# Block 2's mixer: two steps of the delta rule in turns 7 to 11, the end reordered, and products of constants in front of TensorE's waits

## Time and profile before

| | us |
|---|---|
| median of 3 executions | 3647.48 (3641.82 to 3655.58) |
| the profiled execution: its time | 3662.31 |
| its span, first to last instruction | 3660.5 |
| TensorE (PE) busy | 3531.4 |
| VectorE (DVE) busy | 2143.4 |
| ScalarE (ACT) busy | 1253.5 |
| GpSimd (POOL) busy | 699.6 |
| mixer of block 2, pass 1 and pass 2 | 153.9 and 143.9 |

### The profile page before, as it was taken

The page is one execution under the profiler, slowest core; times in us unless marked ns, Lnnn a source line. Parts: engine busy times, 40 slices in busy tenths (PEclk is TensorE's granted clock), DMA queues, the critical chain, the costliest instruction groups (busy, mean ns, idle before and its releaser), DMA issues. The chain is left out here.

```text
span 3660.5 us, 43323 instructions
## 1 busy us (share of the span) xinstructions
PE 3531.4 (96%) x17650; PEld 2759.1 (75%) x17650; DVE 2143.4 (59%) x2908; ACT 1253.5 (34%) x1836; POOL 699.6 (19%) x414
## 2 busy tenths in 40 slices
PE   8999998999999999998999999999999999999999
PEld 6888743788878888744888877686888876768887
DVE  6655556765475556557755577674544565745444
ACT  3222235422243223235422244344222343542221
POOL 3342002244304341002344205100000020000000
PEclk9999999999999999999999999998999999999999
DMA  5443301343433443211444322101233321012332
GB/s 178 142 133 124 106 28 36 135 138 130 133 100 127 136 139 114 91 44 53 139 141 133 124 81 76 35 14 64 87 101 97 96 81 35 14 65 86 101 101 81
DMA packets 97957, 351.16 MB, mean 96 GB/s; under 512 B 11808, under 2 KB 12064, under 8 KB 96864
## 3 DMA queue, kind: packets, MB, share of 16 engines
q1 hardware_dynamic: 97760, 348.40, 29.1%
HBM read 345.86 MB, written 2.42 MB: 95 GB/s over the span
## 5 line engine op out<-in xcount | busy, mean ns | idle before, releaser
L417 ACT ACTIVATE w_hi<-raw 128x1024 fp32r<-128x1024 f32 (+2 forms) x538 | 556.5, 1037 | 1810.5 <-PE ps L336 1727.2
L334 PE MATMUL ps<-xs_hi,w_hi 128*128 128x512 f32 x2304 | 908.0, 394 | 2.5 <-DVE arena L1304 2.5
L336 PE MATMUL ps<-xs_hi,w_lo 128*128 128x512 f32 x2304 | 900.4, 391 | 0.0
L335 PE MATMUL ps<-xs_lo,w_hi 128*128 128x512 f32 x2304 | 900.4, 391 | 0.0
L427 DVE TENSOR_TENSOR w_lo<-raw,w_hi 128x1024 fp32r<-128x1024 f32 (+2 forms) x538 | 673.5, 1253 | 167.9 <-ACT w_hi L417 167.4
L334 PEld LDWEIGHTS ps<-xs_hi,w_hi 128*128 128x128 f32 x2304 | 434.9, 189 | 105.7 <-issue 15.4
L335 PEld LDWEIGHTS ps<-xs_lo,w_hi 128*128 128x128 f32 x2304 | 434.7, 189 | 93.3 <-issue 3.6
L336 PEld LDWEIGHTS ps<-xs_hi,w_lo 128*128 128x128 f32 x2304 | 434.7, 189 | 91.0
L334 PE MATMUL ps<-hd_hi,w_hi 128*128 128x512 f32 x1280 | 500.9, 391 | 2.1 <-DVE hd_lo L1041 2.1
L336 PE MATMUL ps<-hd_hi,w_lo 128*128 128x512 f32 x1280 | 498.7, 390 | 0.0
L335 PE MATMUL ps<-hd_lo,w_hi 128*128 128x512 f32 x1280 | 498.5, 389 | 0.0
(11 more groups left out here) (479 smaller groups left out, 4200.9 us busy)
## 6 DMA issues: line engine op xcount, KB each, us to landing
raw<-in_ffn_gu SPq DMA_DIRECT2D x264, 512.0 KB, 3.8
arena<-in_ada SPq DMA_DIRECT2D x64, 768.0 KB, 5.7
raw<-in_ffn_dn SPq DMA_DIRECT2D x96, 448.0 KB, 3.4
raw<-in_in_t SPq DMA_DIRECT2D x60, 512.0 KB, 3.6
raw<-in_ffn_dn SPq DMA_DIRECT2D x48, 512.0 KB, 3.6
raw<-in_out SPq DMA_DIRECT2D x32, 512.0 KB, 3.6
raw<-in_pleg SPq DMA_DIRECT2D x16, 512.0 KB, 3.6
raw<-in_in_r SPq DMA_DIRECT2D x8, 512.0 KB, 3.6
```

Of the source, the lines that this page charges most:

```text
L334: T.matmul(bank, lhs_hi(k), rhs_hi(k), start=(first and k == 0), stop=False)
L335: T.matmul(bank, lhs_hi(k), rhs_lo(k), start=False, stop=False)
L336: mm = T.matmul(bank, lhs_lo(k), rhs_hi(k), start=False, stop=(last and k == kt - 1))
L417: A.activation(self.hi[:, n % HL, 0:size], raw[:, n % RAW, 0:size], ACT.Copy).then_inc(self.high_done, 1)
```

## The change

1. `weave` takes two delta steps instead of one in each of turns 7 to 11, on all engines. From turn 12 on delta step t + 5 stands in turn t, so the recurrence stands in turns 20 to 27 instead of 25 to 32, and the weave ends after turn 30 (ScalarE's and VectorE's last unit), not 32.
2. Head pairs of the HGRN output are issued alternately (heads 0 and 1 of a pair, product by product) in two turns, 27 and 28, instead of four.
3. `idle_products(bank, n)` multiplies constants into a free PSUM region. It is added after attention units 0 and 2 (512 columns), before levels 9 to 13 (256 columns), before the last z and before U and W (512 columns), and before each chunk's `v_ready` wait (384 columns).
4. The four spreads of steps 2 and 4 are issued before the wait for `kb_ready`.
5. The last chunk's state product and state update are dropped; the state is not used after it.
6. ScalarE: the copies and squares of the HGRN outputs move in front of the SiLUs, which become its last work of the stage; `ring.high` moves up. The squares of the delta output are made chunk by chunk in the mixer (into `o_sq`), so `LateDelta` has no squares left to make. VectorE's `ring.low` calls come one turn earlier.

```diff
-            T.matmul(bank, C("ident"), cst[:, 0:S], start=True, stop=True)
+            T.matmul(bank, C("ident"), cst[:, 0:bank.shape[1]], start=True, stop=True)
...
+    TWICE = range(7, 12)
     def weave(first, second):
         live = [first, second]
+        turn = 0
         while live:
             live = [g for g in live if next(g, DONE) is not DONE]
+            if turn in TWICE:
+                next(first)
+            turn += 1
...
+                    if m in (0, 2):
+                        idle_products(ps[3][:, :], 1)
...
                 for g in range(len(steps)):
-                    pe.wait_ge(x_ready, 2 * g + 3)
...
                     if g >= 2:
                         pe.wait_ge(lev_copied, 2 * (g - 2) + 2)
+                    if g >= 9:
+                        idle_products(ps[2 * (g % 2)][:, 2 * P:S], 1)
+                    pe.wait_ge(x_ready, 2 * g + 3)
...
-                for hd in range(H):
-                    c, e = divmod(hd, 2)
-                    if e == 0:
-                        pe.wait_ge(off_copied, 8 if c else 5)
...
+                for c in range(2):
+                    pe.wait_ge(off_copied, 8 if c else 5)
+                    pair = [(2 * c + e, ps[c][r, :]) for e, r in enumerate(heads_of)]
+                    v_ = lambda hd, j: vn[:, j, P + hd * HD:P + (hd + 1) * HD]
+                    for hd, out in pair:
+                        T.matmul(out[:, 0:P], v_(hd, 0), diag[:, hd, 0, :], start=True, stop=True)
+                    for hd, out in pair:
+                        T.matmul(out[:, P:2 * P], v_(hd, 0), off[:, hd, 0:P], start=True, stop=False)
...
+                    mm.then_inc(o_done, 1)
                     yield
...
             def hgrn_act(act):
...
+                ring.high(act, n0)
                 yield
-                yield
+                act.wait_ge(z_done, 2 * (NL - 1))
+                for c in range(2):
+                    ring.high(act, n0 + 1 + c)
+                    act.wait_ge(o_done, c + 1)
+                    A.activation(hg[:, c, :], ps[c][:, :], ACT.Copy).then_inc(o_copied, 1)
+                    act.wait_ge(o_copied, c + 1)
+                    A.activation(hg_sq[c], hg[:, c, :], ACT.Square)
+                    yield
                 act.wait_ge(lev_done, 4 * NL)
                 for c in range(2):
                     A.activation(hg_gates[:, c, :], bg[:, c, :], ACT.Silu)
                     A.activation(cgt[:, c, :], cgt[:, c, :], ACT.Silu)
-                yield
...
             def hgrn_dve(dve):
...
-                for _ in range(4):
+                for _ in range(3):
                     yield
                 for c in range(3):
                     ring.low(dve, n0 + c)
...
             def delta_pe(pe):
...
                     pe.wait_ge(nat_copied, 4)
-                    pe.wait_ge(kb_ready, 2)
                     if c:
                         pe.wait_ge(head_ready, 4)
                     for e in range(2):
                         T.matmul(ps[6 + e][:, :], pick(4, 2 * c + e), rowG[R4, :], start=True, stop=True).then_inc(spread, 1)
+                    pe.wait_ge(kb_ready, 2)
...
+                        if v == NL - 1:
+                            idle_products(ps[6][:, :], 1)
...
+                idle_products(ps[4][:, :], 1)
                 pe.wait_ge(t_updated, 2 * NL)
...
+                    idle_products(ps[6][:, P:S], 1)
                     pe.wait_ge(v_ready, 2 * j + 2)
...
-                    for hd in range(H):
-                        mm = T.matmul(ps[6][heads_of[hd % 2], (hd // 2) * HD:(hd // 2 + 1) * HD], kdec[:, j, hd * HD:(hd + 1) * HD],
-                                      vnew[:, hd, :], start=True, stop=True)
-                    mm.then_inc(k_done, 1)
+                    if j < ST - 1:
+                        for hd in range(H):
+                            mm = T.matmul(ps[6][heads_of[hd % 2], (hd // 2) * HD:(hd // 2 + 1) * HD], kdec[:, j, hd * HD:(hd + 1) * HD],
+                                          vnew[:, hd, :], start=True, stop=True)
+                        mm.then_inc(k_done, 1)
...
             def delta_act(act):
...
                      .then_inc(out_copied, 1)
+                    act.wait_ge(out_copied, j + 1)
+                    A.activation(o_sq[:, :, j * P:(j + 1) * P], o[:, :, j * P:(j + 1) * P], ACT.Square)
...
             def delta_dve(dve):
...
                     yield
+                    if j == ST - 1:
+                        break
                     dve.wait_ge(k_done, j + 1)
```

More of the change, by code:

```diff
@@ L1079, in program, with __init__ @@
     class LateHeads:
-        def __init__(self, st, x, gains, space, squared=0):
-            self.norms = HeadNorms(st, "late_head", x, gains, HD, space, ps[0], squared=squared)
+        def __init__(self, st, x, gains, space, squares=None):
+            self.norms = HeadNorms(st, "late_head", x, gains, HD, space, ps[0], squares=squares)
             self.gate_ready, self.ready = st.sem("late_gate"), st.sem("late_ready")
@@ L2130, in program, with __init__ @@
     class HeadNorms:
-        def __init__(self, st, tag, x, gains, width, space=None, bank=ps[6], after=None, squared=0):
+        def __init__(self, st, tag, x, gains, width, space=None, bank=ps[6], after=None, squares=None):
             self.x, self.gains, self.width, self.n, self.bank = x, gains, width, len(x), bank
-            self.squared = squared
+            self.squared = len(squares) if squares else 0
             self.squares_before = after.squares_before + after.n - after.squared if after else 0
-            self.sq, self.root, self.rstd = ((space.get(len(x), S), space.get(S), space.get(S)) if space
-                                             else (head_sq, head_root, head_rstd))
+            self.sq = squares or [a[:, r, :] for a in (space.get(len(x), S) if space else head_sq,) for r in range(len(x))]
+            self.root, self.rstd = (space.get(S), space.get(S)) if space else (head_root, head_rstd)
             self.rows = slice(0, 2 * self.n)
@@ L2713, in hgrn_pe @@
                     yield
-                for hd in range(H):
-                    c, e = divmod(hd, 2)
-                    if e == 0:
-                        pe.wait_ge(off_copied, 8 if c else 5)
[L2718 to L2726, removed]
-                    mm = T.matmul(out[:, 3 * P:S], v_(3), diag[:, hd, 3, :], start=False, stop=True)
-                    if e:
-                        mm.then_inc(o_done, 1)
@@ new lines, in hgrn_pe @@
+                for c in range(2):
[6 more added lines that the diff above has]
+                        T.matmul(out[:, P:2 * P], v_(hd, 0), off[:, hd, 0:P], start=True, stop=False)
+                    for hd, out in pair:
+                        T.matmul(out[:, P:2 * P], v_(hd, 1), diag[:, hd, 1, :], start=False, stop=True)
+                    for hd, out in pair:
+                        T.matmul(out[:, 2 * P:S], v_(hd, 0), off[:, hd, 2 * P:4 * P], start=True, stop=False)
+                    for hd, out in pair:
+                        T.matmul(out[:, 2 * P:S], v_(hd, 1), off[:, hd, 4 * P:6 * P], start=False, stop=False)
+                    for hd, out in pair:
+                        T.matmul(out[:, 2 * P:3 * P], v_(hd, 2), diag[:, hd, 2, :], start=False, stop=False)
+                    for hd, out in pair:
+                        T.matmul(out[:, 3 * P:S], v_(hd, 2), off[:, hd, P:2 * P], start=False, stop=False)
+                    for hd, out in pair:
+                        mm = T.matmul(out[:, 3 * P:S], v_(hd, 3), diag[:, hd, 3, :], start=False, stop=True)
+                    mm.then_inc(o_done, 1)
@@ L3118, in _ @@
                 weave(delta_dve(dve), overlapped(window_dve(dve), hgrn_dve(dve)))
-        return X_AT + 6 * S, hg, hg_gates, o, cgt
+        return hg_sq + [o_sq[:, c, :] for c in range(2)], X_AT + 8 * S, hg, hg_gates, o, cgt
     one_half = [0.5] * DT
```

19 lines of the change are left out of this document (5 added, 14 removed).

## The result

The changed kernel takes 3661.2 us (median of 19 runs, 3650.9 to 3666.4), the kernel before 3649.8 (19 runs, 3641.8 to 3658.2). The ratio is 1.0026, with a 95% interval of 1.0019 to 1.0033: about 10 us slower, and the interval leaves out 1. That is under the half percent that the prediction called no change, and inside its range, 3 us under the upper end. Ratios leave out executions that ran at a low clock throughout: there were two, both of the kernel of experiment 10. The profiled execution of the changed kernel took 3659.65 us with a span of 3657.9.

The account below looks back on a forecast made before the run. TensorE bounds it (busy 3531.4 of 3660.5 us). Turn 2 -4.8 and pass 1 without its fall -10.9 give -15.7; falls +12 each, at one and a half +2.3: 3649, no change. Own range 3637 to 3662; with rivals 3626 to 3664.

Parts of the forecast that it names:

- Turns 7 to 11, to W, to the sums: Mixer stretches per pass: 34.1 us, then 31.4 to the end of W (fall adds 12), then 33.9 to the sums.
- The wait in turn 16: TensorE idles 1.65 us before the level in turn 16, as VectorE's delays from GpSimd's copies and a scaling add.
- I take three of four: Share of passes whose clock falls in turns 17 to 19, costing 12 us each.
- The prediction's line for two falls, +8.3: Both mixer passes together, if the clock falls in both: 8.3 us slower than before.
- the idle time of 1.06 led to a fall: Turn 21 before the change: this wait led to a fall in one of two passes; 1.65 should more often.
- Turn 2: Spreads moved ahead remove VectorE's waits for the scores, 2.21 and 2.60 us: -4.8 us over both passes.
- I cost them at nothing: Two products of constants near turn 2, 0.89 us each, taken as covered; if not, +1.8 us a pass.
- The output pairs: HGRN output: four heads take some 4.8 us, not 8.8, but the gain lands behind ScalarE; TensorE idles 5.6.
- 99.4 against 99.4: nothing: Pass 2 from turn 7 to the sums of squares: 99.4 us before and after, no gain.
- Rival 1: 512-column products carry the clock over the half steps; neither pass falls: -19.3 us, 3628; chance 0.20.
- Rival 2: Low clock lasts past W to the off-diagonal products, +10 us a pass more: 3676, or 3664 with one pass; chance 0.10.
- Rival 3: Output pairs don't overlap, each pass loses 3.3 us: +8.9, 3656; chance 0.07.

Follow-up runs that it names:

- experiment 10: Kernel before with one full product of constants (512 columns) ahead of the level's wait in turn 21: 3647.2 us, ratio 0.9993.
- experiment 11: Changed kernel with 1.56 us of full products ahead of turn 16's wait, SiLUs a turn before the copies, no constants in turns 0 and 2: 3631.1 us.
- experiment 5: Changed kernel without the products of constants in turns 0 and 2 of the window attention: 3642.2 us in two groups, ratio 0.9993.
- experiment 3: Changed kernel with VectorE's four output scalings in units 6, 8, 9 and 10 instead of 6 to 9: 3652.6 us, ratio 1.0011.
- Experiment 1: Changed kernel with three full products of constants (256 columns) at the level in turn 16; they ran behind the idle time: 3643.4 us, ratio 0.9981.
- experiment 7: Changed kernel without any of its added products of constants: 3647.4 us, ratio 0.9990.
- experiment 2: Changed kernel with three products of constants in turn 16, cut to 64 rows and 64 columns of TensorE: 3667.1 us, ratio 1.0046.
- experiment 4: Changed kernel with ScalarE's four SiLUs one turn before the copies of the off-diagonal products, not as its last work: 3653.3 us, ratio 0.9998.
- experiment 12: Experiment 11's kernel with scalings moved, one 512-column product in turn 16, products in turn 6's wait and at the stage's end: 3620.7 us, ratio 0.9921.
- Experiment 6: Changed kernel with one delta step in every turn (TWICE emptied), all other parts kept: 3633.7 us, ratio 0.9956.

## Why the prediction was right, and where it was not

**Turns 7 to 11, to W, to the sums: right.** 33.3 against 34.1; the idle time left is 0.5 us, as I took it, and the five added steps cost 1.9 us each and not 2.09 (TensorE's busy time rose from 23.2 to 32.8). With a fall 41.4 and 42.0 against 43.4; 34.5 and 35.0 against 33.9 (the terms of that sum, as printed, add to 34.1). From turn 7 on both passes take 109.76 us against 111.4. A fall costs 10.5 to 11.1 (30.89 of experiment 11 taken from 41.43 and 41.97; 11.1 within experiment 5), not 12.

**The wait in turn 16: right** in place, releaser and size (1.60 for 1.65), and in its two parts (experiment 3).

**How often the clock falls: too low, and the main miss of size.** "I take three of four": it was both passes in the profile, and of the 19 runs the fastest, 3650.9, is the size of one fall below the median. The prediction's line for two falls, +8.3, is near what the stretches show (+7.0), in part by luck: two misses cancel. Turn 2 gave 2.7 us in the two passes where 4.8 was taken, and the rest of the mixers grew by 9.7 where the prediction has 13.1. The rest of the 11.5 us between the medians lies in the reference: the prediction added to the median of before as if it held one fall. With 286.9 us for two mixers without a fall (297.8 less the prediction's 10.9) and 304.8 after, a difference of 11.5 leaves 6.4 us of falls in the median run of before, some 0.6 of one. That is an estimate; the profiles of the three kernels with the old order of those turns show falls in three of six passes.

**The wait as the cause: half wrong.** The prediction's step was "the idle time of 1.06 led to a fall", so that 1.65 "should do it more often". Experiment 1 kept the wait of 1.60 us and had no fall; experiment 7 had one pass with 1.62 us and none. What goes with the fall is the wait followed by a level and a half step with no full product between: both passes fell in the profiles of the changed kernel and of experiments 2 and 4, one of two in experiments 5 and 7, and one of two with the wait at 1.0 us (experiment 3); none of six where full products stand there (experiments 1, 11, 12). Two passes a kernel are few: whether a shorter wait makes the fall rarer is not shown, though experiment 3's median is in line with it. And why one pass of a program falls and the other does not stays open.

**Turn 2: half.** VectorE's wait for the scores went in pass 1 from 2.21 to 0.89 us and in pass 2 altogether, but the stretch gained 1.7 and 1.0 us, not 2.4 each. The step that failed is "I cost them at nothing": the product of turn 2 stands ahead of what VectorE wants next. The prediction had the price for that case, 0.9 each; at half clock it is 1.9.

**The output pairs: right.** 4.35 us for four heads (4.8 predicted), behind ScalarE, whose SiLUs were the last work; 5.50 us idle for 5.6. Experiment 4 gives the tail's price: TensorE's wait before the sums is 3.35 us shorter in each pass.

**"99.4 against 99.4: nothing": right as a sum, and it hid the finding.** It is the whole change against the kernel before, and less the fall the measured passes give 98.7 to 99.2. I never set the change against itself without its doubled steps. Experiment 6 does: the other parts save some 4 us a pass and keep the clock, and the two steps a turn cost 12.4 us a pass and 1.6 at the sums. They put the half steps behind a longer wait with no product of constants there, and they leave the output pairs as TensorE's last work, so that ScalarE's copies and SiLUs have nothing beside them. At the full clock they gain nothing: 98.7 to 99.2 us from turn 7 on, against 97.2 with one step a turn.

**The rivals.** Rival 1, the clock holds, was not what happened, and experiment 1 shows how near it was: one place for a full product. Rival 2 is out: the clock is back with the end of W in both passes (the level behind it takes 1.11 us). Its figure for one pass, 3664, does not follow from its own terms, which give 3666 (3647.5 + 8.3 + 10). Rival 3 is out by L2737.

**The number.** The forecast was 3649, no change. The time of 3661.2 is 12 us above it, and the difference of 11.5 from before is clear of noise where 1.5 was forecast. That it lies in the range is owed to the range's width, which the falls and the rivals set.

## What to carry to other kernels

Before moving work on an engine that seems full, ask what each wait is followed by: here a wait before narrow products cost 10 us in most passes, and the same wait before full ones cost its own length. Filler belongs ahead of the longest wait, and the wait instruction to put it ahead of is the one that the trace names. When a change has several parts and the sum is nothing, work out each part against the rest of the change, not only the whole against before; and do not make activations that need a new table the last work of a stage when they can stand beside TensorE's work (3.35 us a pass here).

## What was not expected of the hardware

- TensorE was busy 5.00 of 5 us at a granted clock of 0.50, and stayed at 1.2 GHz for 24 us in all. Three products on 64 rows and 64 columns did not keep it from falling; three on the whole array, as long in time and in the same place, did (experiments 1 and 2).
- The same wait (1.6 us) and the same half step fall in some passes and not in others of one program (experiments 5 and 7).
- GpSimd's copies double VectorE's two-operand work in SBUF (0.41 to 0.83 us), and leave its copies out of PSUM as they are (L3059, 0.73 us beside them and 0.76 ahead of them). The Trainium skill says in "GPSIMD Engine Reference", section 1, "Specifications", that the two share their SBUF interfaces and contend where VectorE has two SBUF inputs; the trace agrees.
- Two 64-column halves of TensorE work side by side: two f32 products of 256 columns, one in each half, take 0.43 us from start to start, where one took as long.
